# GpSimd makes the high half of float32 weights by a rounding copy instead of adding zeros, with its loops over units written out

## What is computed

```python
D_MODEL = 1024; SEQ = 1024; DEC_BATCH = 8; DEPTH = 2; D_FF = 2816
def swiglu(h, wg, wu, wd):
    return (jax.nn.silu(h @ wg) * (h @ wu)) @ wd
# hybrid_mixer:  _split(h @ w_in, ...) -> retention, gated delta -> mixed @ w_out
# ssm_mixer:     _split(h @ w_in, ...) -> conv, SSD -> yg @ w_out
# each: x = x + mixer(rmsnorm(x)); x = x + swiglu(rmsnorm(x))
```

## Time and profile before

| | us |
|---|---|
| median of 3 runs | 3465.35 (3461.84 to 3466.01) |
| the profiled execution's own time | 3463.11 |
| its span, first to last instruction | 3461.2 |
| TensorE matmul busy | 3209.8 (93%), 20050 matmuls |
| VectorE busy | 1663.6 (48%) |
| ScalarE busy | 782.7 (23%) |
| GpSimd busy | 1208.0 (35%) |
| mean granted TensorE clock | 0.975 |

### The profile page before, as it was taken

The page is one execution under the profiler, slowest core; times in us unless marked ns, Lnnn a source line. Parts: engine busy times, 40 slices in busy tenths (PEclk is TensorE's granted clock), DMA queues, the critical chain, the costliest instruction groups (busy, mean ns, idle before and its releaser), DMA issues.

```text
span 3461.2 us, 47065 instructions
## 1 busy us (share of the span) xinstructions
PE 3209.8 (93%) x20050; PEld 3074.6 (89%) x20050; DVE 1663.6 (48%) x1899; ACT 782.7 (23%) x1115; POOL 1208.0 (35%) x528
## 2 busy tenths in 40 slices
PE   6999888988789999999987999999987999999997
PEld 5898788888779999999977897988976999999997
DVE  6343656565552222222386858768686322232224
ACT  4212324224240000000044414233144100000002
POOL 2222302112024343343333545446462343433432
PEclk9999999999999999999999999999998999999998
DMA  4111101001011111111112213122130111111111
GB/s 142 68 50 62 41 25 38 32 29 40 14 36 43 49 49 43 49 43 49 43 40 77 95 55 116 50 94 83 61 119 31 47 43 49 45 48 49 43 49 62
DMA packets 79236, 190.76 MB, mean 55 GB/s; under 512 B 20900, under 2 KB 36932, under 8 KB 78920
## 3 DMA queue, kind: packets, MB, share of 16 engines
q1 hardware_dynamic: 52384, 150.03, 12.9%
q10 hardware_dynamic: 26664, 37.88, 3.4%
HBM read 164.07 MB, written 19.59 MB: 53 GB/s over the span
## 4 chain that ended last, share of the span: by engine, by line
PE 78%; DVE 12%; issue 4%; ACT 3%; POOL 1%; DMA 1%; ACTq 0%; DVEq 0%; SPq 0%; POOLq 0%
PE ps_set L551 64%; PE ps_core L823 4%; PE ps_set L560 2%; PE ps_core L1015 2%; ACT work L1079 1%; DVE work L1802 1%; DVE work L1594 1%; DVE work L1918 1%; PE ps_core L1020 1%; ACT L1079 1%; DVE work L2129 1%; DMA w_raw<-in_w 1%; PE ps_set L635 1%; DVE work L2144 1%; DVE conv_s L1805 1%
## 5 line engine op out<-in xcount | busy, mean ns | idle before, releaser
L475 POOL TENSOR_TENSOR w_hi<-w_raw,small 128x1024 fp32r<-128x1024 f32 x230 | 452.4, 1967 | 2079.5 <-PE ps_set L551 1848.4
L551 PE MATMUL ps_set<-h_hi,w_hi 128*128 128x344 f32 x3696 | 809.6, 327 | 18.2 <-ACT work L1079 14.9
L551 PE MATMUL ps_set<-h_lo,w_hi 128*128 128x344 f32 x3696 | 784.8, 321 | 0.0
L551 PE MATMUL ps_set<-h_hi,w_lo 128*128 128x344 f32 x3696 | 780.8, 320 | 0.0
L551 PEld LDWEIGHTS ps_set<-h_hi,w_hi 128*128 128x128 f32 x3696 | 621.5, 189 | 38.9 <-issue 20.6
L551 PEld LDWEIGHTS ps_set<-h_lo,w_hi 128*128 128x128 f32 x3696 | 625.8, 189 | 0.0
L551 PEld LDWEIGHTS ps_set<-h_hi,w_lo 128*128 128x128 f32 x3696 | 616.3, 188 | 0.0
L478 POOL TENSOR_TENSOR w_lo<-w_raw,w_hi 128x1024 fp32r<-128x1024 f32 x230 | 605.7, 2634 | 18.1
L2016 DVE TENSOR_TENSOR work<-work,ps_set 128x1032 f32<-128x1032 f32 x44 | 54.1, 1229 | 786.8 <-PE ps_set L551 776.9
L1669 DVE TENSOR_TENSOR x<-x,ps_set 128x1032 f32<-128x1032 f32 x160 | 196.7, 1229 | 256.4 <-PE ps_set L551 256.4
L551 PE MATMUL ps_set<-y_hi,w_hi 128*128 128x344 f32 x1296 | 285.1, 329 | 15.8 <-ACT work L1079 7.5
(11 more groups left out here) (219 smaller groups left out, 3519.4 us busy)
## 6 DMA issues: line engine op xcount, KB each, us to landing
w_raw<-in_w SPq DMA_DIRECT2D x230, 512.0 KB, 3.3
work<-ssm_cum_rows ACTq DMA_DIRECT2D x32, 512.0 KB, 4.3
sample<-in_ssm_state SPq DMA_DIRECT2D x16, 512.0 KB, 4.2
out_ssm_s<-sample SPq DMA_DIRECT2D x16, 512.0 KB, 2.6
x<-in_x SPq DMA_DIRECT2D x6, 688.0 KB, 15.2
work<-work ACTq DMA_DIRECT2D x16, 258.0 KB, 2.4
out_y<-x SPq DMA_DIRECT2D x6, 688.0 KB, 3.4
sample<-bc_rows SPq DMA_DIRECT2D x8, 512.0 KB, 4.9
```

The lines of the kernel that those rows point to most:

```text
L475: return nc.gpsimd.tensor_tensor(w_hi[:, k, :], w_raw[:, k, :], zeros, ALU.add)
L551: mm = nc.tensor.matmul(out[:, g, 0:TN], w[:, slot, cols], v[:, g * TN:(g + 1) * TN], start=(start and n == 0), stop=(stop and n == 2))
```

## The change

`high` becomes a `tensor_copy` from `w_raw`, which is float32, to `w_hi`, which is fp32r, so that the copy rounds. The broadcast column of zeros goes, and with it GpSimd's wait for the constants. The two loops are replaced by Python loops that write out every split, 172 in all, with their waits on constants. SyncE, TensorE, VectorE and ScalarE have the same program as before.

```diff
         @block.gpsimd
         def _(pool):
-            zeros = ZERO.to_broadcast([P, 1024])
-            pool.wait_ge(consts_in, 48)
-
             def high(k):
-                return nc.gpsimd.tensor_tensor(w_hi[:, k, :], w_raw[:, k, :], zeros, ALU.add)
+                return nc.gpsimd.tensor_copy(w_hi[:, k, :], w_raw[:, k, :])
...
-            with pool.Fori(1, SSM0 // 2) as i:
-                split(i, 0)
-                split(i, 1)
+            for unit in range(2, SSM0):
+                split(0, unit)
             for gr in range(GROUPS):
                 state_space(gr)
             for unit in range(SSM_UNIT["z0", GROUPS - 1] + 6, FFN1):
                 split(0, unit)
-            with pool.Fori(FFN1 // 2, UNITS // 2) as i:
-                split(i, 0)
-                split(i, 1)
+            for unit in range(FFN1, UNITS):
+                split(0, unit)
```

## The result

| | before | changed |
|---|---|---|
| median of 4 runs, us | 3465.68 | 3428.97 |
| range, us | 3461.84 to 3466.24 | 3428.64 to 3429.46 |
| profiled execution, us | 3463.11 | 3429.46 |
| VectorE busy, us | 1663.6 | 1594.0 |
| GpSimd busy, us | 1208.0 | 998.0 |

The ratio is 0.9897 with a 95% interval of 0.9879 to 0.9914: 1.0% faster, some 30 to 42 us. Profile against profile it is 33.65 us. Taken again beside other kernels, the changed kernel stood at 0.9898 (0.9879 to 0.9917).

What follows compares the result with a forecast made beforehand. TensorE was taken as the bound (78% of the chain), waiting in places on VectorE blocked by GpSimd. Six terms summed to 20.4 us off 3463.1 us, 3442.7 us, or 3445.0 us against the median; range 3433 to 3469 us.

Steps and rivals of the forecast that it cites:

- waits for the low half: TensorE waiting directly for a low half at starts of stages: four of five places counted, 0.74 us each, 3.0 us.
- norms: Norms between stages, VectorE blocked ahead of TensorE's waits: one split in three places, two in two, 5.2 us.
- scalars of the two mixers: VectorE's scalar chains at 401 us (0.7 us) and from 1783 us on (two splits, 1.5 us).
- ends of the state space groups: Three group ends, VectorE blocked in two splits each ahead of TensorE's wait of 2.47 us: 4.5 us gained.
- inside the groups, four waits: Inside state space groups, L1801 and the copy behind it lose a split ahead of TensorE's 1.61 us waits: 3.0 us.
- gated delta heads: Four heads where L1889, blocked by the low half, stands ahead of TensorE's waits: 2.5 us.
- The copy's price: GpSimd's high half as a copy: 1.15 us in place of 1.893 us, 0.74 us less per split.
- Start, loops, fetch of code: Kernel start, written-out loops and fetching the longer program: each claimed to change the time by nothing.
- dearer copy: Rival: the copy costs what the two-input form does, 14 us lost, 3479 us; chance 0.08.
- no change: Rival: copy costs about the addition, or ScalarE and DMAs give the freed time back; 3465 us, chance 0.19.
- order at the lock: Rival: a shorter high half lets the low half lock out L2178's additions, some 1.7 us each; 3475 us, chance 0.05.
- The cover that the prediction named: The 2.57 us of idle time of L2175 behind L2178, said to cover the addition's delay of some 1.7 us.

Runs made afterwards that it cites:

- the kernel with the loops alone: Every split written out, the addition of zeros kept, against the kernel before: 3464.17 us, ratio 1.0002.
- the kernel with nine copies: Loops written out, copy in nine splits at the first three state space group ends, addition elsewhere, against the kernel before: 3453.84 us, ratio 0.9972.
- the kernel with the stored ones: Kernel before with the high half as w_raw times a stored tensor of ones in place of w_raw plus zeros: 3476.38 us, ratio 1.0042.

## Why the prediction was wrong

The direction and the mechanism were right: a shorter high half frees VectorE where TensorE waits for it. The step that failed is the count of splits in VectorE's chains. 20.4 us were forecast, 33.65 us lie between the profiles, and the median of 3428.97 us is 4 us below the range. TensorE's idle time, forecast and then measured, place by place (us):

| place | forecast | measured |
|---|---|---|
| waits for the low half | 3.0 | 5.0 |
| norms | 5.2 | 4.2 |
| scalars of the two mixers | 2.2 | 2.2 |
| ends of the state space groups | 4.5 | 7.5 |
| inside the groups, four waits | 3.0 | 2.9 |
| gated delta heads | 2.5 | 2.6 |
| places left out | 0 | 3.6 |
| sum | 20.4 | 28.0 |

The measured sum is 28.0 us of the 29 us by which the idle time fell. Taking each place by its own row:

- *The copy's price.* 1.15 us was taken, 1.042 us measured, d = 0.85 in place of 0.74. On the same list this is 20.4 x 0.85 / 0.74 = 23.4 us, 3 us more. The ratio of VectorE's forms was a usable guide. The 0.88 us and 1.54 us that the prediction worked out from the Trainium skill ("GPSIMD Engine Reference") are the one below the measurement and the other far above it; between 512 and 1024 columns the copy's rate, 0.84 ns a column, is nearly the 0.86 ns that the first stands for.
- *Ends of the state space groups: the term that failed.* 4.5 us forecast, two splits at each of three ends. The chain runs through three: L2135, the third, was left out, and its four executions shrank from 3.01 to 1.87 us as a group. With three splits at d = 0.85 the whole waits go, and they did: 7.5 us of idle time, some 7 us by the kernel with the loops alone. The stretches became 10 us shorter (3.8 + 3.9 + 2.3), and the kernel with nine copies 9.9 us faster; the 3 us between fit the clock behind two of the waits, which the step did not count. Seven of twelve such ends in the profiles have no such fall, so that part is in good measure luck of the profiled execution.
- *The same count elsewhere.* At 401 us one split was counted and the wait shrank by 1.35 us, not 0.7: L1695 at 393.58 us was in the chain too. "The last group's waits I leave out" left out one split at L2135 (2.92 us before), and TensorE's wait there went from 18.32 to 17.09 us. Four waits of 0.6 us on L2067 inside the groups, not on the list, are gone, 2.4 us. All of these are the same in the repeated profile of the changed kernel.
- *Inside the groups and the gated delta heads.* The four waits of 1.61 us: 3.0 us forecast, 6.4 to 3.5 us measured. Waits on L1894 (now L1889): 2.5 us forecast, 3.8 to 1.2 us measured. Both right.
- *How the list was made.* I walked the gaps for stretched instructions and took an instruction's shortest execution for its undisturbed one, by form and line. L1889 warned of that, since all four of its executions were blocked. The chain from its start to its end would have shown every split in it. Two other waits look shorter in the changed kernel's profile, one on ScalarE at 430 us (2.85 to 2.22 us) and one on VectorE's L1625 at 950 us (5.28 to 4.16 us); in the repeated profile they are 3.28 and 5.27 us, so they vary from one execution to the next and are no part of the account.
- *Direct waits.* 3.0 us from four places forecast; all five, 5.0 us, are gone, the one of 1.6 us by more than d. The fifth was left out on the ground that VectorE sets that stretch. Its 0.9 us of idle time did go, but whether the end moved by it was not tested apart.
- *Norms.* 5.2 us forecast for 7 splits. At 965, 1712, 3411 and 2671 us 0.81, 0.79, 0.86 and 1.43 us were measured: about d a split, as put. At 1738 us two splits were counted, and the two waits together shrank by 0.3 us only (2.78 and 2.99 to 1.94 and 3.56 us). The scalars of the second mixer gave 0.9 us (1.73 to 0.85 us at 1808 us) of the 1.5 us forecast; that the two mixers together come to the 2.2 us forecast is luck.
- *Start, loops, fetch of code: nothing*, as forecast: the split of unit 2 stands at 58.3 us in both, and written-out loops alone give 1.0002.
- *The range.* Its low end varied d and kept the list. The list itself was the weaker part. With the cases of an incomplete list it should have gone some 10 us lower.

Of the rivals, the dearer copy and "no change" fell with the 1.042 us. The order at the lock came true in its first half. L2178 (now L2173), changed:

```profile
2003.24 3.44 DVE L2173 TENSOR_TENSOR x<-x,work 128x1032 f32<-128x1032 f32 x1
2007.64 1.23 DVE L2170 TENSOR_TENSOR work<-work,ps_set 128x1032 f32<-128x1032 f32 x1 [0.96 <-PE ps_set L546]
```

1.83 us became 3.44 us, since the subtraction has the port now, and VectorE's idle time behind it went from 2.57 to 0.96 us. The cover that the prediction named held, with 0.96 us left.

What stays open: the gated delta stage, from the split of unit 20 to that of unit 43, took 645.7 us before and 642.6 to 648.9 us in four kernels whose high half there also lasts 1.89 us, against 637.8 us in the changed kernel and 638.1 us in its repeat. So the 8 us that it gained are settled to some 3 us only. The remaining difference between idle time (29 us) and span (34 us) is TensorE's busy time. Most of it is the clock: in the state space stage TensorE ran at 1.2 GHz for 47.8 us before and for 41.0 us in the changed kernel, which is 3.4 us of work. But the kernel with the loops alone has 37.5 us there, so this too may be the execution and not the change.

## What to carry to other kernels

Look for instructions whose longest execution is far from their shortest, on both engines that share a port, and count a helper engine's instruction not by its own idle time but by whom it makes stand. Then measure the whole chain that an engine waits for, from its first instruction to its last, and count every split that it runs through: an instruction that was long and is short again may only have handed its loss to the next one. The wait shrinks by the shortening once for each such meeting, and no further than to nothing. Compare two executions of the same kernel before a difference of a single wait is called an effect. When a range is set, put the whole list of such places in doubt, not only the price of one.

## What the runs showed of the hardware

- On GpSimd a float32 to fp32r copy of 128x1024 takes 1.042 us, 128x768 0.828 us, 128x512 0.613 us: 0.84 us per 1000 columns and some 0.18 us fixed. A memset of 128x1024 takes 0.954 us, a float32 addition 1.893 us with a broadcast or with the same tensor twice. With two inputs that differ a subtraction takes 2.34 us or more, and so does a product whose second input is 128 columns read eight times over (2.337 us at least, 2.399 us median).
- VectorE's instructions with two inputs in SBUF are held up by GpSimd's additions (L1575 at 965 us, 2.45 us for 0.88), subtractions (L1797, 3.30 us for 1.28) and copies (L1803, 1.02 us for 0.18), but not by its memset (1.23 us beside it). VectorE's copy of 8 columns is held up by the subtraction (2.37 us for 0.16) and by the memset (1.01 us); its tensor_scalar of 128x1024 by the addition (2.38 us for 0.74) and, in one case at 429 us, by the memset (1.47 us).
- TensorE's waits of 2.67 and 2.47 us at two of the three group ends were followed by 3.4 us at 1.2 GHz, the one of 2.38 us at the third was not. The length of the wait alone does not decide it: in other runs a wait of 2.34 us was followed by such a fall, and three of 3.12 to 3.14 us (the kernel with the stored ones) were not. Removing the wait gained 3.8 and 3.9 us where the clock had fallen, and 2.3 us where it had not.
